# A mixture over 16,384 experts: rows gathered by token, or both tables through TensorE whole

## What is computed

```python
def short_conv_mixer(xn, w_in, conv_w, w_out):
    bg, cg, hx = jnp.split(xn @ w_in, 3, axis=-1)
    y = causal depthwise conv of width 3 over (cg * hx)
    return (bg * y) @ w_out

def peer(xn, w_q, sub_keys, u, v):
    q = (t @ w_q).reshape(n_tok, PEER_HEADS, 2, PEER_DKEY // 2)
    sc = jnp.einsum('thpd,hpnd->thpn', q, sub_keys)
    s1, i1 = lax.top_k(sc[:, :, 0], 16); s2, i2 = lax.top_k(sc[:, :, 1], 16)
    top_s, pos = lax.top_k(all 256 sums s1 + s2, 16)
    eidx = (i1 * 128 + i2) at pos;  gate = jax.nn.softmax(top_s, axis=-1)
    hid = gelu(einsum('td,thkd->thk', t, u[eidx]))
    return einsum('thk,thkd->td', gate * hid, v[eidx])

for layer in range(2):
    h = h + mixer(rmsnorm(h)); h = h + peer(rmsnorm(h), ...)
return rmsnorm(h)
```

## Time and profile before

| | before |
|---|---|
| median of 3 runs | 2208.86 us (2207.1 to 2209.22) |
| span of the profiled execution | 2205.8 us |
| the same execution lies around the median | 3.1 us under it |
| TensorE busy, share of the span | 1846.9 us, 84% |
| VectorE busy | 1313.2 us, 60% |
| ScalarE / GpSimd busy | 483.7 us, 22% / 677.8 us, 31% |
| DMA moved | 766.74 MB, mean 348 GB/s |

### The profile page before, as it was taken

One profiled execution on the slowest core, in us unless ns is written; L12 is line 12 of the kernel. 1 busy time (PEld: TensorE's weight loads), 2 busy tenths in 40 slices (PEclk: granted clock), 3 DMA queues, 4 the chain that ended last, 5 costly groups with the idle time before them and its releaser, 6 DMA issues.

```text
span 2205.8 us, 18976 instructions
## 1 busy us (share of the span) xinstructions
PE 1846.9 (84%) x5842; PEld 878.5 (40%) x5842; DVE 1313.2 (60%) x3353; ACT 483.7 (22%) x1212; POOL 677.8 (31%) x593
## 2 busy tenths in 40 slices
PE   9999998998899968888768877778887767888876
PEld 4445554333244544444223333323333433334422
DVE  1343423211033357767777878897688798777665
ACT  1232321111011213222221222222121221222221
POOL 2010001111000034434443434554334445444442
PEclk9999999999999989999999989989999998999999
DMA  7433239999773299999999999999999999999996
GB/s 258 153 120 105 105 129 372 414 418 419 284 292 134 73 394 384 421 420 422 421 421 421 376 421 421 419 409 422 421 421 420 391 422 420 422 421 416 422 419 260
DMA packets 112152, 766.74 MB, mean 348 GB/s; under 512 B 15840, under 2 KB 16528, under 8 KB 20528
## 3 DMA queue, kind: packets, MB, share of 16 engines
q0 software_dynamic: 78928, 542.37, 59.8%
q1 hardware_dynamic: 30528, 213.07, 24.4%
q10 hardware_dynamic: 2592, 10.04, 1.2%
HBM read 767.52 MB, written 10.49 MB: 353 GB/s over the span
## 4 chain that ended last, share of the span: by engine, by line
DMA 31%; DVE 18%; issue 10%; PE 9%; POOL 4%; ACT 1%; DVEq 0%; POOLq 0%; ACTq 0%
DMA arena<-in_c_rows_dram,arena 30%; DVE arena L2626 7%; POOL arena L2711 4%; PE banks L313 4%; DVE x L2636 2%; PE banks L2287 2%; PE banks L1904 1%; PE banks L2612 1%; DVE arena L2519 1%; DVE arena L2522 1%; DVE arena L2557 1%; DVE arena L2528 1%; DVE arena L2561 1%; DVE arena L2566 1%; PE banks L344 0%
## 5 line engine op out<-in xcount | busy, mean ns | idle before, releaser
L2612 PE MATMUL banks<-arena 128*128 128x512 f32 x1784 | 879.3, 638 | 279.6 <-ACT arena L2693 274.7
L2711 POOL DMA_INDIRECT arena<-in_c_rows_dram,arena x512 | 599.4, 1171 | 806.5 <-PE banks L2612 537.5
L2626 DVE CUSTOM_DVE_ANT_0 arena<-arena,xn 128x1024 f32<-128x1024 f32 x512 | 624.5, 1222 | 255.7 <-DMA arena<-in_c_rows_dram,arena 254.1
L2612 PEld LDWEIGHTS banks<-arena 128*128 128x128 f32 x1784 | 343.2, 202 | 763.0 <-ACT arena L2693 379.1
L313 PE MATMUL banks<-ring,hT 128*128 128x512 f32 (+1 forms) x672 | 284.3, 578 | 0.0
L2693 ACT ACTIVATE arena<-ident,small 128x128 f32<-128x128 f32 x446 | 158.3, 395 | 545.0 <-DVE small L2633 532.0
L313 PEld LDWEIGHTS banks<-ring,hT 128*128 128x128 f32 x672 | 123.3, 190 | 141.2 <-issue 139.1
L375 ACT COPY arena<-banks 128x512 f32<-128x512 f32 (+4 forms) x211 | 97.2, 488 | 337.9 <-PE banks L359 147.5
L2684 ACT ACTIVATE small<-small 128x2 f32<-128x2 f32 x256 | 52.2, 204 | 486.6 <-DVE small L2626 486.5
L401 POOL TENSOR_TENSOR small<-small 128x1 f32<-128x1 f32 (+4 forms) x24 | 34.3, 1431 | 353.0 <-DVE small L397 330.7
L380 DVE COPY arena<-banks 128x512 f32<-128x512 f32 (+1 forms) x45 | 30.4, 678 | 145.1 <-PE banks L1354 70.8
(11 more groups left out here) (310 smaller groups left out, 1664.2 us busy)
## 6 DMA issues: line engine op xcount, KB each, us to landing
arena<-in_c_experts_dram SPq DMA_DIRECT2D x53, 1024.0 KB, 25.2
ring<-in_c_experts_dram SPq DMA_DIRECT2D x33, 1024.0 KB, 22.0
ring<-in_c_w_in_dram SPq DMA_DIRECT2D x30, 1024.0 KB, 4.9
ring<-in_c_odd_w_in_dram SPq DMA_DIRECT2D x19, 1024.0 KB, 9.0
ring<-in_c_w_q_dram SPq DMA_DIRECT2D x18, 1024.0 KB, 9.3
ring<-in_c_even_w_in_dram SPq DMA_DIRECT2D x14, 1024.0 KB, 7.6
arena<-in_c_rows_dram,arena POOLq DMA_INDIRECT x512
ring<-in_c_odd_w_out_dram SPq DMA_DIRECT2D x8, 1024.0 KB
```

Source lines behind the costliest of these rows:

```text
L2612: r = e.matmul(banks[:, bank_of[("acc", L, c, hf)], :], diag[:, diag_of[m], :], rows[:, m % NB, D + hf * 512:D + (hf + 1) * 512], start=fi ...
L2626: e.tensor_tensor_reduce(u, u, xn[:, c, :], 1.0, 0.0, ALU.mult, ALU.add, hid3[:, c, h, k:k + 1]).then_inc(ve.sem, ve.up(("u", p)))
L2711: e.indirect_dma_start(rows[:, b, :], None, table_uv, bass.IndirectOffsetOnAxis(ap=eix[:, c, 16 * h + k:16 * h + k + 1], axis=0)).then_inc ...
```

## The change

Nothing is gathered any more. In each layer both tables pass through the core whole, in 128 tiles each of 128 experts x 1024 (512 KB). The tile number `j` is the first key of its experts, the place in the tile the second key.

- `pe_pair` (L2313): for each `u` tile eight matmuls, the tile's 128x128 blocks as weights and the 256 tokens (both chunks) as the moving operand, so 128 experts x 256 tokens come out; ScalarE applies gelu to two tiles at a time (`act_pair`) into `hid`, which holds all 16,384 x 256 values.
- The choices for both chunks are made by VectorE first (`dve_choose`, then `dve_keys` for 8 heads at once). Token numbers are turned into a gate matrix in 32 groups of 8 tokens: VectorE makes two one-hot matrices from the keys (`dve_hot`), ScalarE multiplies one by the gates (`act_hot`, eight instructions 128x128), TensorE multiplies the two (`pe_group`, L2339, eight matmuls 128x128), and VectorE multiplies `hid` by the result (`dve_group`). 37 of the 64 pairs of `u` tiles (`BEFORE`) come before the first group, 27 are spread between the groups; those are weighed later (`dve_weighed`).
- `pe_values` (L2354): for each `v` tile four matmuls of 512 columns, with `hid` as weights.
- The odd mixer (`pe_odd`) takes both chunks at once, 256 tokens wide, after layer 0 has ended, with its weights in the arena; no PEER work lies beside it.
- GpSimd issues no indirect DMA in this part. The `u` and `v` tiles go over the SP queue into six and ten places of 512 KB. The sixth weight slot moves from `ring` to the arena. The host lays out `u` transposed in blocks.

```diff
-            e.indirect_dma_start(rows[:, b, :], None, table_uv,
-                                 bass.IndirectOffsetOnAxis(ap=eix[:, c, 16 * h + k:16 * h + k + 1], axis=0)).then_inc(
-                                     row_in[b].sem, row_in[b].up(("uv", m), by=16))
...
-                r = e.matmul(banks[:, bank_of[("acc", L, c, hf)], :], diag[:, diag_of[m], :],
-                             rows[:, m % NB, D + hf * 512:D + (hf + 1) * 512], start=first, stop=last)
...
+        def pe_pair(e, L, i):
...
+            for j in (2 * i, 2 * i + 1):
+                s = j % NST_U
+                e.wait_ge(st_in[s].sem, st_in[s].at(("u", L, j)))
+                for k in range(8):
+                    r = e.matmul(banks[:, i % 4, T * (j % 2):T * (j % 2) + T], st[s][:, P * k:P * (k + 1)], hT[:, k, :],
+                                 start=(k == 0), stop=(k == 7))
+                r.then_inc(pe.sem, pe.up(name))
...
+            e.wait_ge(ac.sem, ac.at(("hot", L, g)))
+            for t in range(GROUP):
+                b = 4 + 2 * (g % 2) + t // 4
+                r = e.matmul(banks[:, b, P * (t % 4):P * (t % 4 + 1)], hotB[g % 2][:, t, :], hotA[g % 2][:, t, :],
+                             start=True, stop=True)
...
+                for hf in range(2):
+                    r = e.matmul(banks[:, 4 + 2 * c + hf, :], hid[:, j, P * c:P * (c + 1)],
+                                 st[s][:, 512 * hf:512 * (hf + 1)], start=(j == 0), stop=(j == P - 1))
...
+            for i in range(BEFORE):
+                pe_pair(e, L, i)
+                if i == 22:
+                    pe_keys(e, L, 0)
+            for g in range(NGROUP):
+                pe_group(e, L, g)
+                for i in pairs_after(g):
+                    pe_pair(e, L, i)
+                if g == 6:
+                    pe_keys(e, L, 1)
+            pe_values(e, L)
...
+            for s_, dst in ((1, hotB[g % 2]), (0, hotA[g % 2])):
+                e.tensor_tensor(dst, iota128.unsqueeze(1).to_broadcast([P, GROUP, P]),
+                                idxT[:, s_, t0:t0 + GROUP].unsqueeze(2).to_broadcast([P, GROUP, P]),
+                                ALU.is_equal).then_inc(ve.sem, ve.up(("hot", L, g)))
...
+            w = hid[:, 0:n, t0:t0 + GROUP]
+            e.tensor_tensor(w, w, v[:, 0:n, :], ALU.mult).then_inc(ve.sem, ve.up())
+            e.tensor_copy(hid[:, n:P, t0:t0 + GROUP], v[:, n:P, :]).then_inc(ve.sem, ve.up(("G", L, g)))
```

More of the change, by code:

```diff
@@ L2070, in vector_even @@
             ve.mark("even")
-            moment[0] = "first"
-            for _ in dve_choose(e, 0, 0, 0):
-                pass
+            dve_joined(e, 1, 0)
+            dve_joined(e, 1, 512)
+            dve_norm(e, "ffn20", 1)
+            dve_turned_chunk(e, "ffn20", 1)
         def act_ret_square(e, c):
@@ L2152, in build @@
[L2152 to L2190, removed]
@@ L2193, in build @@
[L2193 to L2252, removed]
@@ L2253, in build @@
-        put(2 * SEG + 20, "gain", "fin", "mix1")
-        norm_steps(3 * SEG + 4, "fin", 0)
-        def sync_peer(e):
[L2257 to L2268, removed]
-                    if what[0] == "out" and what[3] % 4 == 0:
-                        _, c, hf, k = what
-                        load(e, ("oddout", c, hf, k), w_odd_out[2 * hf + k // 4])
[L2272 to L2275, removed]
+            pool_norm(e, "ffn20", 1)
@@ new lines, in pe_group @@
+        def pe_group(e, L, g):
+            for i in range(2):
+                before = take_at(("G", L, g, i), 4 + 2 * (g % 2) + i)
+                if before is not None:
+                    e.wait_ge(*emptied[before])
+            e.wait_ge(ac.sem, ac.at(("hot", L, g)))
[3 more added lines that the diff above has]
+                             start=True, stop=True)
+            r.then_inc(pe.sem, pe.up(("G", L, g)))
@@ L2395, in pe_beside @@
-            if kind == "sc":
-                _, c, h = what
-                b, before = rings.take(("sc", 1, c, h))
-                if before is not None:
-                    e.wait_ge(*emptied[before])
-                e.wait_ge(fetched("kt1").sem, fetched("kt1").at("all"))
-                e.wait_ge(ac.sem, ac.at(("q", 1, c, h)))
-                for f in range(2):
-                    r = e.matmul(banks[:, b, f * P:(f + 1) * P], qp[h % 2][:, f * P:(f + 1) * P], kt[:, 2 * h + f, :],
-                                 start=True, stop=True)
-                r.then_inc(pe.sem, pe.up(("sc", 1, c, h)))
@@ L2504, in build @@
-        moment = [0]
+                    for k in range(8):
+                        if k % 4 == 0:
+                            s = odd_out_landed[2 * hf + k // 4]
+                            e.wait_ge(s.sem, s.at("all"))
+                        if c == 0 and hf == 0:
+                            e.wait_ge(ve.sem, ve.at(("y", k)))
+                        r = e.matmul(banks[:, b, :], yT[:, k, P * c:P * (c + 1)], odd_out[2 * hf + k // 4][:, k % 4, :],
+                                     start=(k == 0), stop=(k == 7))
```

782 lines of the change are left out of this document (411 added, 371 removed).

## The result

The changed kernel takes 2954.45 us (median of 4 runs, 2952.47 to 2957.04), the kernel before 2209.04 us on the same chip (4 runs, 2207.1 to 2210.77): a ratio of 1.3372, interval 1.3353 to 1.3391. The prediction was 2952 us (2910 to 3030). The profiled run has a span of 2950.6 us at a mean granted clock of 0.994.

What follows compares the result with a forecast made beforehand. The prediction took the kernel before to be bound by its gathers and the changed one by TensorE's own stream; its steps along TensorE summed to 2949 us, plus 3.1 for the median of runs: 2952 us, range 2910 to 3030.

Steps and rivals of the forecast that it cites:

- 4: norm: Between layer 0's last `v` product and the odd mixer: two additions, then square to first product, 6.5 us, formerly hidden.
- 5: odd mixer: After layer 0's norm: 83 us, then 27.5 us of TensorE records, with nothing running beside it.
- Two records at the old pitch: Table and gate products: each fp32 matmul leaves two records, 0.429 us at 512 columns; 938 us a layer, 1876 in all.
- Waits in the group stage: TensorE waiting for ScalarE's one-hots at group 0 (3.4 us), group 1 (1) and four more (1.6 each): 11 us a layer.
- What hides: Behind TensorE's products: tile feed at 153 to 190 GB/s, choices of 142 us a layer, VectorE's and ScalarE's group work.
- Steps 1 and 2: Even mixer's product ending at 776.6 us as before, then layer 0's remaining heads, to 844 us.
- Step 6: Layer 1's heads, 8 x 4.9 + 35.4 + 2 x 1.9 + 1 = 79 us, the second norm hidden behind chunk 0's.
- The tail: From the end of the last product to the end of the span, as before: 11 us.
- Half price: Rival: table products take what a single record now takes, 2050 us in all, a gain; chance 2%.
- Strides: Rival: strided weighing makes VectorE bind the group stage, +20 or +154 us a layer, 2990 or 3260; over 3020, 5%.
- Clock under unbroken work: Rival: granted clock falls to 0.95 through both layers, +95 to 100 us, 3050 us; chance 6%.
- Late feed: Rival: tiles arrive at half of the 153 GB/s needed, +900 us; chance 1%.

Runs made afterwards that it cites:

- e1: Changed kernel without chunk 1's value products for the first 120 of 128 `v` tiles of each layer, every load kept: 2541.39 us.
- e2: Changed kernel without loads of `u` tiles behind the first 6 and `v` tiles behind the first 10 of each layer: 2953.68 us.
- e3: Changed kernel with all 64 pairs of `u` tiles ahead of the groups, none between them: 3116.61 us.
- e10: Changed kernel with chunk 0's gate exponentials on ScalarE behind pair 8 in place of pair 13: 2953.38 us.
- e4: Changed kernel with the operands of both tables' products read as bf16 (upper halves of the fp32 words), same loads and order: 1927.16 us.
- e7: Kernel before, with gathers of 4 KB a row instead of 8 and both products reading this half row: 2004.39 us.
- e8: Kernel before, without one of the two value products of each position, but for the first and last of each chunk: 2208.15 us.

## Why the prediction was right

Its steps against the changed kernel's trace, in us:

| step | predicted | measured |
|---|---|---|
| 1, 2: first tile of `u`, layer 0 | 844 | 841.8 |
| 3: layer 0, first tile to last product | 949 | 950.7 |
| 4: norm | 6.5 | 6.6 |
| 5: odd mixer | 110.5 | 112.0 |
| 6: layer 1's heads | 79 | 81.8 |
| 7: layer 1 | 949 | 950.7 |
| 8: tail | 11 | 7.0 |
| span | 2949 | 2950.6 |

- **Two records at the old pitch.** This carried 1876 of the 2949 us and held: the counts above, and 412 us in e1. `u` and groups with their waits took 511.1 us in layer 0 (841.75 to 1352.81), where 442 + 57 + 11 are 510, and `v` 439.6, where it was 439.
- **Waits in the group stage.** 11 us a layer predicted, 8.3 measured (3.1 for group 0 where I had 3.4, 10.4 in both layers for eight waits of 1.3, where I had four of 1.6 a layer). The size is right and the releaser is not: I had those four down to ScalarE's one-hots, and in the trace they end with VectorE (L2549), which has to empty the banks of an earlier group. That the two sizes agree is luck. Nor did group 1 wait the 1 us that I gave it. Instead the records of groups 0 and 1, right behind the first wait, are slow: 32 in 5.54 us, where 32 of this form take 3.74, 1.8 us that I had not counted.
- **What hides.** Feed (e2), choices and group operands did. The claim that pairs hide ScalarE's one-hots is the one of them with a price: 81 us a layer (e3). VectorE was idle for 65% of the stretch ahead of the groups and for 52% of the one with them, over half as foreseen. But most of the idle time ahead of the groups is waits of 76.77 and 81.87 us for exponentials, which I had not seen. They were covered: the first got shorter in e10 without effect.
- **The heads.** Steps 1 and 2 are 2.2 us too long; the even mixer's last product ended 1.3 us earlier than before (775.35). Step 6 is short by 2.8: a wait of 2.12 for the norm's square where the row of before had 0.83, and the first head at 5.44 us, not 3.7.
- **The tail.** 4 us off: the span ended 3.1 us after the DMA of the last output was issued, before 6.9. That and the first heads made up for 6 of the 7.8 us that the other steps took more, so that the two spans lie only 1.6 us apart owes something to luck.
- **Rivals.** Half price: refuted by the record counts; e4 shows what lower precision gives, and that the sum then ends at the feed. A rule of the Trainium skill stood behind that rival, "TensorE: Matmul & The Clock Gate", section "Back-to-back issue gap". By that rule, which the page gives for a single warm matmul, one of 512 columns takes 216 ns. e4's bf16 records agree with about 0.22 us, and fp32 matmuls at 0.858 us take four such. Strides: 1.218 us, refuted. Clock under unbroken work: 1.00 over 440 us without a gap. Late feed: nothing in e2, and e1 bore 370 GB/s.

So the 745 us are this. From 757 us on the kernel before needed 1449. The changed one needs 85 for layer 0's heads, 2 x 950.7 for the tables, 200 for what stands between them (norm, odd mixer, layer 1's heads, all of which had run in the idle time that the gathers left) and 7 for the tail: 2193, 744 more. It took away a bound by gathers, which lay 206 us ahead of the next (e7), for a bound by TensorE that lies 744 us beyond it.

## What to carry over

Before a gather is replaced by a product over the whole table, hold the table's bytes against the matmul passes it needs: here 512 KB of fp32 took 3.4 us of products for 1.28 us of transfer, so halved bytes ended in a longer time; at one pass the same scheme sits at the feed and wins. Take the price per matmul from the record count and the pitch in the trace of the same dtype, since it decided the whole sum. And when a bound goes away, look at what had been hidden by it, and ask what the next bound is: 206 us in the old scheme, the late keys in the new one.

## What the hardware showed besides

- **The clock eats freed time.** In e8 half the value products went, yet their busy time fell by less than a third, 879.3 us to 627.7: the granted clock was 0.81 on average against 0.95, between the levels of 2.4 and 1.2 GHz, and a record took 825 ns on average instead of 638. Busy time of an engine that waits is not the work it has.
- **Short waits can leave slow records behind them.** The stretches with the groups behind the 3.11 us wait and with the first head behind the norm (clock 0.72 and 0.69):

```profile
1101.00:1104.00 3.00, 3.00 (x20) 2.87 (x20) 0.60 (x1) 2.08 (x8) 0.00 (x0) 0.72 0.00 0
1914.00:1919.50 5.50, 5.40 (x32) 5.28 (x32) 1.42 (x3) 0.00 (x0) 0.03 (x1) 0.69 0.01 3
```

It is not so behind every such wait. In e3 the first group's 16 records, behind a wait of 3.10 us, took 2.02 us, and in e4 the same first head of layer 1, behind the same wait of 2.12 us, took 3.81. What decides it these runs don't show.

```profile
1288.72 2.02 PE L2339 MATMUL banks<-ring 128*128 128x128 f32 x16 [3.10 <-ACT ring L2537]
```

- **Transfers of 512 KB land back to back.** At one every 1.28 us they reach 412 GB/s (e4), as much as the gathers of 8 KB rows did at 406, with no larger transfer needed.
